# Last norm of a decoder layer: token sums on partitions, inverse roots spread by a unit-matrix product, first gate row in halves

## What is computed

```python
f = (jax.nn.gelu(uc + ffn_conv_b, approximate=True) * gt) @ w_ffn_down
x = x + rmsnorm(f, g_ffn_post)       # the last norm: over the 2048 channels of each token
x = x + jax.nn.sigmoid(x @ w_ple_gate) * (p @ w_ple)
```

## Time and profile before

| | |
|---|---|
| median of 3 runs | 2653.61 us (2653.44 to 2654.08) |
| time of the profiled execution | 2653.8 us |
| its span | 2652.0 us |
| TensorE busy | 2642.8 us, 100% |
| VectorE busy | 2223.5 us, 84% |
| ScalarE busy | 1386.6 us, 52% |
| last FFN down product ends, gate's first matmul starts | 2467.87 us, 2474.20 us |

### The profile page before, as it was taken

One profiled execution on the slowest core, in us unless ns is written; L12 is line 12 of the kernel. 1 busy time (PEld: TensorE's weight loads), 2 busy tenths in 40 slices (PEclk: granted clock), 3 DMA queues, 4 the chain that ended last, 5 costly groups with the idle time before them and its releaser, 6 DMA issues.

```text
span 2652.0 us, 55404 instructions
## 1 busy us (share of the span) xinstructions
PE 2642.8 (100%) x20929; PEld 2582.7 (97%) x20929; DVE 2223.5 (84%) x3908; ACT 1386.6 (52%) x2530; POOL 190.0 (7%) x289
## 2 busy tenths in 40 slices
PE   9999999999999999999999999999999999999999
PEld 8999999999999999999999999999999999999899
DVE  7988888888896687898888888888888768789987
ACT  6544545555563255655555555555555454445354
POOL 0221000000010000000000000000000000000000
PEclk9999999999999999999999999999999999999999
DMA  6676434333474455655566655665569575565674
GB/s 229 187 209 183 136 114 142 132 128 118 158 256 159 133 165 156 250 171 164 170 202 187 187 154 167 190 206 169 157 195 309 152 249 165 161 204 170 238 263 152
DMA packets 159884, 479.59 MB, mean 181 GB/s; under 512 B 17161, under 2 KB 51217, under 8 KB 156336
## 3 DMA queue, kind: packets, MB, share of 16 engines
q1 hardware_dynamic: 128608, 370.74, 39.8%
q0 software_dynamic: 30960, 106.59, 18.2%
q10 hardware_dynamic: 144, 0.15, 0.0%
HBM read 420.56 MB, written 55.71 MB: 180 GB/s over the span
## 4 chain that ended last, share of the span: by engine, by line
PE 96%; DVE 2%; issue 1%; ACT 1%; DMA 0%; SPq 0%; DVEq 0%; ACTq 0%
PE pair L1190 78%; PE pair L1155 6%; PE pair L1293 3%; PE pair L1271 3%; PE pair L1093 2%; PE pair L925 1%; PE pair L1250 1%; PE pair L1115 1%; PE pair L977 1%; PE pair L998 1%; DVE v_lo L1917 0%; DVE lo L2266 0%; PE pair L987 0%; PE pair L1058 0%; DMA s_raw<-in_sstream 0%
## 5 line engine op out<-in xcount | busy, mean ns | idle before, releaser
L1190 PE MATMUL pair<-o_hi,v_hi 128*128 128x260 f32 x5832 | 1653.9, 284 | 1.0 <-DVE v_lo L1917 0.5
L1190 PE MATMUL pair<-o_hi,v_lo 128*128 128x260 f32 x5832 | 1646.7, 282 | 0.0
L1358 ACT ACTIVATE v_hi<-s_raw 128x512 fp32r<-128x512 f32 (+1 forms) x1366 | 850.9, 626 | 937.1 <-PE pair L1190 793.1
L1190 PE MATMUL pair<-lo,v_hi 128*128 128x260 f32 x4164 | 1176.2, 282 | 0.0
L1917 DVE TENSOR_TENSOR v_lo<-s_raw,v_hi 128x512 fp32r<-128x512 f32 (+1 forms) x1286 | 872.8, 681 | 302.8 <-ACT v_hi L1358 265.9
L1190 PEld LDWEIGHTS pair<-o_hi,v_hi 128*128 128x128 f32 x5832 | 1096.5, 188 | 14.3 <-issue 12.1
L1190 PEld LDWEIGHTS pair<-o_hi,v_lo 128*128 128x128 f32 x5832 | 1098.3, 188 | 0.0
L1190 PEld LDWEIGHTS pair<-lo,v_hi 128*128 128x128 f32 x4164 | 782.6, 188 | 0.2
L1190 PE MATMUL pair<-lo_E,v_hi 128*128 128x260 f32 x834 | 236.0, 283 | 0.0
L1190 PE MATMUL pair<-lo_A,v_hi 128*128 128x260 f32 x834 | 235.2, 282 | 0.0
L1358 ACT ACTIVATE v_hi<-s_one 128x512 fp32r<-128x512 f32 (+1 forms) x220 | 137.0, 626 | 186.9 <-PE pair L1190 152.4
(11 more groups left out here) (273 smaller groups left out, 2498.1 us busy)
## 6 DMA issues: line engine op xcount, KB each, us to landing
s_raw<-in_sstream SPq DMA_DIRECT2D x468, 512.0 KB, 5.0
s_one<-in_sstream POOLq DMA_DIRECT2D x168, 512.0 KB, 5.4
raw<-f_scr SPq DMA_DIRECT2D x12, 1040.0 KB, 7.5
s_raw<-in_sstream SPq DMA_DIRECT2D x32, 384.0 KB, 4.1
g_scr<-d_h SPq DMA_DIRECT2D x16, 520.0 KB, 2.7
g_in<-g_scr SPq DMA_DIRECT2D x32, 260.0 KB, 2.8
x_scr<-y_sb SPq DMA_DIRECT2D x8, 1040.0 KB, 4.8
s_one<-in_sstream POOLq DMA_DIRECT2D x16, 384.0 KB, 4.9
```

The source lines that it names most:

```text
L1190: mm = pe.matmul(out, wt[:, slot, kk * P:kk * P + P], r[:, k, :], start=j in (0, 1, 3) and k == 0 and n == 0, stop=k == nk - 1 and n == 2, ...
L1358: nc.scalar.activation(v_hi[:, n % 4, 0:width], src, ACT.Copy, scale=0.5 if halved(u) else 1.0).then_inc(v_hi_rdy, 1)
```

## The change

For the last norm only, the sums are turned: the squares (87 tokens at a time, three spans for each half, the middle span and the last overlapping by one token) are the stationary operand and one column of ones is the moving one, so that token sums lie on 87 partitions and three columns (`token_sums`). ACT takes the root of this 87x3 tile, and DVE inverts it. `spread` brings the values back to 128 partitions: an inverse column, broadcast to 128 columns, is the stationary operand, and an 87x87 part of the unit matrix the moving one. For this a copy of the unit matrix, `spread_id`, is loaded into the place of `fs_s`; SP issues this load after the waits for `ple_stored` and a wait for `f_ready`, ahead of `gate_in(0)`. TensorE waits for it (`tab_ready` 128) before it spreads half 1. The nine fill matmuls become three.

Row 0 (and the products of row 1) is made in halves, half 1 first, and `plain_unit` begins with half 1 of row 0; `xn_rdy` therefore counts one more. Products read the spread values from PSUM. In `plain_unit`, the waits for both weight quarters stand ahead of the row's matmuls. Elsewhere, `rope_sin` and `rope_cos` become one semaphore `rope_mul`.

```diff
+        SPAN = 87
+        SPANS = (0, SPAN, HALF - SPAN)
+        inv = at("inv", [P, 8], o[0])
+        spread_id = at("spread_id", [P, P], o[0] + 64)
...
             for c in range(4):
                 sp.wait_ge(ple_stored[c], 16)
+            sp.wait_ge(f_ready, KF)
+            sp.dma_start(spread_id[:, :], ident_in).then_inc(tab_ready, 16)
             gate_in(0)
             for c in range(4):
-                sp.wait_ge(xn_rdy, KD + 4 * c + 4)
+                sp.wait_ge(xn_rdy, KD + 4 * c + 5)
...
+                    for n, h in blocks if k or s == 2 else [(n, h) for h in (1, 0) for n in range(2)]:
+                        if s == S_GATE and k == 0 and (n, h) == (0, 0):
+                            pe.wait_ge(xn_rdy, KD + 2)
...
+            def token_sums(h, squares, first, last):
+
+                for b, t in enumerate(SPANS):
+                    mm = pe.matmul(pair[2][0:SPAN, h, 504 + b:505 + b], squares[:, t:t + SPAN], ones[:, 0:1],
+                                   start=first and b == 0, stop=last, skip_group_check=True)
+                if last:
+                    mm.then_inc(half_rdy, 1)
+
+            def spread(h):
+
+                pe.wait_ge(inverted, 2 - h)
+                for b, t in enumerate(SPANS):
+                    mm = pe.matmul(pair[2][:, h, t:t + SPAN],
+                                   inv[0:SPAN, 3 * h + b:3 * h + b + 1].to_broadcast([SPAN, P]),
+                                   spread_id[0:SPAN, 0:SPAN], start=True, stop=True, skip_group_check=True)
+                mm.then_inc(half_rdy, 1)
...
-                    half_sums(1)
-                    last_square(1)
-                    for n in range(9):
-                        pe.matmul(pair[3][:, n % 2, 0:HALF], ones[:, :], chan[:, 0:HALF],
-                                  start=True, stop=True)
+                    pe.wait_ge(sq_h_added, added_squares(1, 31))
+                    token_sums(1, sq_acc[:, 1, :], True, True)
+                    token_sums(0, sq_acc[:, 0, :], True, False)
+                    for n in range(2):
+                        pe.matmul(pair[3][:, 1, 0:HALF], ones[:, :], chan[:, 0:HALF], start=True, stop=True)
+                    pe.wait_ge(tab_ready, 16 * 8)
+                    spread(1)
+                    pe.wait_ge(sq_h_rdy, 64)
+                    token_sums(0, sq_h[:, 1, :], False, True)
+                    pe.matmul(pair[3][:, 1, 0:HALF], ones[:, :], chan[:, 0:HALF], start=True, stop=True)
+                    spread(0)
...
+                act.wait_ge(half_rdy, 5 - 2 * h)
+                nc.scalar.activation(inv[0:SPAN, 3 * h:3 * h + 3], pair[2][0:SPAN, h, 504:507], ACT.Sqrt,
+                                     scale=1.0 / D, bias=eps[0:SPAN, :]).then_inc(root_rdy, 1)
...
-            half_invert(5, 1)
-            half_invert(6, 0)
-            st.wait()
-            new_x(C_FFNPOST, 1)
-            dve.wait_ge(xn_rdy, 2 * KD)
+            last_x()
+            dve.wait_ge(xn_rdy, 2 * KD + 1)
```

More of the change, by code:

```diff
@@ L507, in build @@
         xsq_summed = sem("xsq_summed")
-        half_sum_rdy = sem("half_sum_rdy")
+        half_rdy = sem("half_rdy")
+        inverted = sem("inverted")
         root_rdy = sem("root_rdy")
@@ L512, in build @@
         rope_in = [sem(f"rope_in{i}") for i in range(2)]
-        rope_sin = sem("rope_sin")
-        rope_cos = sem("rope_cos")
+        rope_mul = sem("rope_mul")
         rope_done = sem("rope_done")
@@ L1079, in plain_unit @@
                         pe.wait_ge(e, u)
+                blocks = [(n, h) for n in range(2) for h in range(2)]
                 for k in range(nk * 2):
-                    pe.wait_ge((h_rdy, None, u_rdy, None, None, None, xn_rdy)[s],
-                               (KD if s == S_GATE else 0) + (min(k + 1, KD - 2) if s == 2 else k + 1))
+                    if s == 2:
+                        pe.wait_ge(u_rdy, min(k + 1, KD - 2))
+                    else:
+                        pe.wait_ge(xn_rdy, KD + (k + 2 if k else 1))
                     if s == 2 and k >= KD - 2:
                         pe.wait_ge(u_late, k - KD + 3)
[L1085 to L1095, removed]
+                    if k % KH == 0:
+                        for n in range(2):
+                            pe.wait_ge(s_rdy[r % 2][2 * n + k // KH], 16 * (r // 2 + 1))
+                    for n, h in blocks if k or s == 2 else [(n, h) for h in (1, 0) for n in range(2)]:
+                        if s == S_GATE and k == 0 and (n, h) == (0, 0):
+                            pe.wait_ge(xn_rdy, KD + 2)
+                        src = (y_sb[:, k, h * HALF:(h + 1) * HALF] if s == S_GATE
+                               else x_half(k, h))
+                        a, b = (upper, ((0, 0), (1, 0)))[n][h]
+                        mm = pe.matmul(pair[a][:, b, 0:HALF],
+                                       s_raw[r % 2][2 * n + k // KH][:, k % KH * P:(k % KH + 1) * P], src,
+                                       start=k == 0, stop=k == nk * 2 - 1, skip_group_check=True)
                     if k >= 2:
@@ L1221, in half_sums @@
                 pe.matmul(pair[2][:, 1, 0:HALF], ones[:, :], sq_acc[:, 1, :],
-                          start=True, stop=True).then_inc(half_sum_rdy, 1)
+                          start=True, stop=True).then_inc(half_rdy, 1)
                 pe.matmul(pair[2][:, 0, 0:HALF], ones[:, :], sq_acc[:, 0, :],
@@ L1229, in last_square @@
                 pe.matmul(pair[2][:, 0, 0:HALF], ones[:, :], sq_h[:, 1, :],
-                          start=False, stop=True).then_inc(half_sum_rdy, 1)
+                          start=False, stop=True).then_inc(half_rdy, 1)
+            def token_sums(h, squares, first, last):
[11 more added lines that the diff above has]
+                mm.then_inc(half_rdy, 1)
             def ple_tile(t):
@@ L1337, in half_root @@
             def half_root(phase, h):
-                act.wait_ge(half_sum_rdy, 2 * phase + 2 - h)
-                nc.scalar.activation(rstd[:, h * HALF:(h + 1) * HALF], pair[2][:, h, 0:HALF], ACT.Sqrt,
-                                     scale=1.0 / D, bias=eps).then_inc(root_rdy, 1)
+                if phase == 0:
+                    act.wait_ge(half_rdy, 2 - h)
+                    nc.scalar.activation(rstd[:, h * HALF:(h + 1) * HALF], pair[2][:, h, 0:HALF], ACT.Sqrt,
+                                         scale=1.0 / D, bias=eps).then_inc(root_rdy, 1)
+                    return
+                act.wait_ge(half_rdy, 5 - 2 * h)
+                nc.scalar.activation(inv[0:SPAN, 3 * h:3 * h + 3], pair[2][0:SPAN, h, 504:507], ACT.Sqrt,
+                                     scale=1.0 / D, bias=eps[0:SPAN, :]).then_inc(root_rdy, 1)
             def v_high(n):
@@ L1419, in o_high @@
                         act.wait_ge((h_rdy, merged_ready, h2_rdy, None, None, None, xn_rdy)[s],
-                                    (KD if s == S_GATE else 0) + (4 * h + 4 if j == 0 else KH + 4 * h + 4))
+                                    (KD + 1 if s == S_GATE else 0) + (4 * h + 4 if j == 0 else KH + 4 * h + 4))
                     nc.scalar.activation(o_hi[j][:, halves(s, h), :], raw_of(s, j)[:, halves(s, h), :],
@@ L1970, in sine @@
                 dve.tensor_tensor(rope_s[r % 2][:, :], rope_s[r % 2][:, :], sin[:, :], ALU.mult)\
-                   .then_inc(rope_sin, 1)
+                   .then_inc(rope_mul, 1)
             def cosine(r):
@@ L1975, in cosine @@
                 dve.wait_ge(rope_in[r % 2], 64 * (r // 2 + 1))
-                dve.tensor_tensor(src, src, cos[:, :], ALU.mult).then_inc(rope_cos, 1)
+                dve.tensor_tensor(src, src, cos[:, :], ALU.mult).then_inc(rope_mul, 1)
             def turn_q(r):
@@ L1980, in turn_q @@
                 dst = src if r < KA else kT_sb[:, BLK:BLK + T]
-                dve.wait_ge(rope_cos, r + 1)
-                dve.wait_ge(rope_sin, r + 1)
+                dve.wait_ge(rope_mul, 2 * r + 2)
                 dve.tensor_tensor(dst, src, rope_s[r % 2][:, :], ALU.add).then_inc(rope_done, 1)
@@ L2730, in new_x, with last_x, token_invert, gain @@
                 add(KD - 1)
+            def last_x():
+                def token_invert(h):
+                    dve.wait_ge(root_rdy, 6 - h)
+                    dve.reciprocal(inv[0:SPAN, 3 * h:3 * h + 3], inv[0:SPAN, 3 * h:3 * h + 3])\
+                       .then_inc(inverted, 1)
+                def gain(k):
+                    return chan[:, C_FFNPOST + k:C_FFNPOST + k + 1]
+                def half_product(k, h):
+                    row = y_sb[:, k, h * HALF:(h + 1) * HALF]
+                    return dve.scalar_tensor_tensor(out=row, in0=row, scalar=gain(k),
+                                                    in1=pair[2][:, h, 0:HALF], op0=ALU.mult, op1=ALU.mult)
+                def half_add(h):
+                    row = y_sb[:, 0, h * HALF:(h + 1) * HALF]
+                    dve.tensor_tensor(row, row, x_tile(0)[:, h, :], ALU.add).then_inc(xn_rdy, 1)
+                def product(k):
```

(21 more changed lines are left out.)

## The result

| | before | after |
|---|---|---|
| median | 2653.98 us (6 runs, 2653.44 to 2654.26) | 2665.34 us (6 runs, 2663.77 to 2666.30) |
| span of the profiled execution | 2652.0 us | 2664.1 us |
| mean granted clock | 1.000 | 0.996 |

The ratio is 1.0043, with a 95% interval from 1.0033 to 1.0053: the change makes the kernel 11.4 us slower. The forecast was 2662.5, with a range to 2665.5; three of the six runs lie above it.

The account below looks back on a forecast made before the run. TensorE, busy 2642.8 of 2652.0 us, was taken to bound the kernel. A late load (7.45 us) and slow restart (1.4) make 8.9: span 2660.9, profiled time 2662.7, median 2662.5 us, range 2659.5 to 2665.5.

Parts of the forecast that it names:

- The mark: Row 1's start in the gate, 2475.95 us before the change; any shift of it reaches the end in full.
- The load's place: `spread_id` in SP's queue behind four weight loads: lands at 2478.4 us, wanted at 2469.4, so TensorE stands 9 us.
- What is queued behind the wait: Last norm's remaining chain starts only after the landing: 5.0 us to row 1, at 2483.4, a loss of 7.45 us.
- The clock: TensorE's stand of 9 us before the gate drops its clock; slow restart costs 1.4 us, bounds nothing to 3 us.
- the row of the span's end: Last 3.9 us without matmuls read clock 1.00; basis of the rival that the clock stays up: 2661.1 us, chance 0.27.
- The price of 1.4 us: Slow restart after the stand, priced from the span's first 14 ones matmuls, 421 ns each against 274 after.
- the sign that I had named: In the changed profile, slower first spread and gate matmuls or clock 0.50 for some 3 us; row 1 starts at 2483 to 2486.
- The sum: Whole kernel: 7.45 us lost to row 1 plus 1.4 for the clock make 8.9; median 2662.5 us.
- the small operations: Between landing and row 1: spreads 0.7 us each, token sums 0.5, root 0.25, inverse 0.18; upper bound allows 0.5 more.
- the longer low clock: Upper end of the range: the restart after the wait costs 3 us in place of 1.4.
- What costs nothing: Inversions shrink from 3.43 us to twice 0.18 and nine fills go, but under the wait; no gain with the late load.
- the rival worked out for a load that isn't late: `spread_id` lands early enough: row 1 starts at 2474.35, 1.6 us earlier, 2652.0 us; chance 0.10.

Follow-up runs that it names:

- the filled run: The changed kernel, its load still late, with 24 fill matmuls instead of 2 ahead of TensorE's wait for `spread_id`; 2663.35 us, ratio 1.0036.
- The early load: The changed kernel with the `spread_id` load issued at the start of the FFN down products; 2652.72 us against 2653.81 for the kernel before, ratio 0.9995.
- the whole-row run: The changed kernel with early load, row 0 made whole and `plain_unit` waiting for whole rows; 2655.68 us, or 2653.90 with three fills behind the last spread.
- the version with the sums first: The changed kernel with early load, one fill, last square's sums ahead of both spreads, row 1 summed right after row 0; 2653.10 us, ratio 0.9997.

## Why the prediction was right

- **The mark.** That nothing behind row 1 absorbs a delay held: the first unit ended 12.1 us later, and the span is 12.1 us longer. The time of the median moved by 11.4.
- **The load's place.** The step held: the load landed 0.2 us behind the fourth weight load. The landing was forecast for 2478.4 and was 2480.16, outside my bounds of 2477.6 to 2479.2 by 1 us. The late issue is not what moved it. The residual piece in front of the weights, issued before them, already took longer to land, 8.8 us from 2466.02 where it took 7.3 from 2465.75 (before, then after):

```profile
L751 SPq DMA_DIRECT2D raw<-x_scr x1: 360/360/360, 2465.7 to 2465.7; - x1
...
DMA to landing us min/median/max: 7.3/7.3/7.3
```
```profile
L755 SPq DMA_DIRECT2D raw<-x_scr x1: 360/360/360, 2466.0 to 2466.0; - x1
...
DMA to landing us min/median/max: 8.8/8.8/8.8
```

Behind it the four weight loads landed 1.28 us apart in both, though the first issue took 2.13 us in one and 0.76 in the other. The step that was mis-sized is the backlog of SP's queue, which I read off a single execution. There the fourth weight load landed 10.3 us after the end of the product; in the eleven other profiled executions it was 11.2 to 12.6 (11.8 in the changed kernel). Why the backlog differs from execution to execution stays open.
- **What is queued behind the wait.** The sums of the last square, half 0's root (ACT waited 13.4 us for it) and VectorE's products began only after the landing, as said. At full clock, from landing to row 1, 5.0 us were forecast; the filled run shows 5.4 (2478.72 to 2484.11).
- **The clock.** It fell, as by the rule of the Trainium skill (TensorE: Matmul & The Clock Gate, "HAM oscillation — how this bites in real kernels"); the row of the span's end, where 3.9 us of no work read 1.00, misled and was no evidence. The price of 1.4 us, taken from the span's start, was too small: 2.5. I had taken the low stretch as 3 us, and it lasted 8 from the landing, through both spreads, the last sums and row 0, which began 4.5 us after it. So row 1 began at 2488.1 (the 26.57 us from its start to the unit's end taken back from 2514.66), and not at 2483 to 2486, the sign that I had named. At full clock VectorE sets the start of row 1, as I had summed it; at half pace the chain from the landing on is TensorE alone.
- **The sum.** 7.45 and 1.4 were forecast for the end of the first unit. 1.8 more for the landing, 1.1 for the clock and 0.4 for the small operations make 12.15, and 12.14 was measured (2502.52 to 2514.66). The three are taken from the same traces, so that they add up is bookkeeping and no second proof; and 0.3 of the landing's 1.8 is the product itself, which ended at 2468.14 instead of 2467.87. The mechanism was right, and three of its terms were small, all to one side. That the range held the median, by 0.2 us, is luck in part: its upper end is reached only when a late landing (0.8), the longer low clock (1.6) and the small operations (0.5) are all added to 2662.5; with the "or" that I wrote between the first two it would be 2664.6, under what was measured.
- **What costs nothing.** The early load shows the rival worked out for a load that isn't late: forecast 1.6 us below before, measured 1.1 in the medians and 1.2 in the traces. But I had put the gain on the inversions, 3.43 against 0.36 us; the whole-row run shows that these are spent again on the spreads, the sums and the fills in front of them, and that the halves make the gain.

That the load's place is the cause is shown by moving it early, moving it 2 MB forward, moving it to another queue, and adding it alone to the old norm. That it is a share of the full DMA engines which keeps ScalarE's queue from being faster than 5 us is argued from the GB/s, not shown. What kept a stand of 1.9 us from passing without a fall of the clock is not shown either; that fills in its place keep the clock at 1.00 is.

## What to carry to other kernels

A small load that an engine will wait for costs the depth of the queue at the place where it is issued, not its size: 64 KB took 2.3 us behind two small stores and 10 us behind a residual piece and four weight loads. Read the depth from more than one execution: here it differed by over 2 us. When you shorten a chain, look for what it newly waits for, and issue that where the queue is empty. And where TensorE must stand for even 2 us next to thin matmuls, fill the time: here the fall of the clock cost as much as the stand.

## What the runs showed of the hardware

- The clock fell after stands of 1.9 and 2.2 us that lie among matmuls of one or 87 columns. In the kernel before, with nine fills between stands of 0.44 and 0.32 us, every run beside these experiments has a mean clock of 1.000. In the version with the sums first, whose kept trace has a stand of 0.9 us, six runs of eleven have 0.999; no trace of such a run was kept, so that fall is read from the mean only. A fall cost 1.9 to 2.5 us in the traces, and not more after a stand of 10 us (2.5) than after one of 1.9 (2.3).
- SP's queue was served in order and at a steady pace: each 512 KB weight load landed 1.28 us behind the one before, and the 64 KB 0.2 us behind the last, in the kernel before and in the changed one alike, though the issues took 0.4 to 2.1 us. In the early-load run, where one issue took 2.79 us, one of the gaps is 1.6.
- A load from ScalarE's queue overtook what stood in SP's: issued at the same moment, the same 64 KB took 5.0 us from the one and 8.7 from the other, behind a residual piece.
- The granted clock in the rows isn't a sure sign at the edges of a span: it read 1.00 at the start, beside matmuls of 421 instead of 274 ns. The spreads of 87 columns show the same step where the rows do tell the two levels, 1.00 in the filled run and 0.50 in the changed kernel:

```profile
L1254 PE MATMUL pair<-spread_id,inv x12: 275/275/342, 2478.8 to 2481.2; 87*128 87x87 f32 x12
```
```profile
L1254 PE MATMUL pair<-spread_id,inv x12: 353/421/516, 2480.2 to 2484.4; 87*128 87x87 f32 x12
```
